# Routing inside the output projection, expert rows scattered per token tile: one change to a Trainium2 hybrid-encoder kernel

## What is computed

```python
def reference(x, meta_tokens, ...):            # x: (1, 1024, 1024) f32, 16 meta tokens in front
    z = rmsnorm(h, attn_norm)
    q, k, v, f_logit, xc, b_gate, c_gate = split(z @ w_in)
    attn = forgetting_attention(q, k, v, f_logit)      # 8 heads of 64
    conv = b_gate * short_conv(c_gate * xc)
    mixed = rmsnorm per group of 64 (concat(attn, conv)) * mix_norm
    h = h + mixed @ w_out
    z = rmsnorm(h, ffn_norm)
    # hierarchical router: top-1 of 4 groups, then top-2 of its 8 experts
    g_prob = softmax(z @ w_rg + b_rg); g_idx = argmax; g_w = max
    top_p, top_i = top_k(softmax((z @ w_re + b_re) of group g_idx), 2); top_p /= sum
    # each expert: (silu(x @ w_gate[e]) * (x @ w_up[e])) @ w_down[e], for the tokens sent to it
    h = h + sum over the two experts of g_w * top_p * expert(z)
    return rmsnorm(h, final_norm)[:, 16:]
```

## Time and profile before

| | |
|---|---|
| median of 3 runs | 1336.21 us (1335.02 to 1337.71) |
| the profiled execution, its own time | 1335.58 us |
| its span, first to last instruction | 1333.8 us |
| PE busy | 1167.0 us, 87% of the span |
| DVE busy | 874.3 us, 66% |
| ACT busy | 737.1 us, 55% |
| POOL busy | 138.8 us, 10% |
| mean granted TensorE clock | 0.95 of full |

### The profile page before, as it was taken

The page is one execution under the profiler, slowest core; times in us unless marked ns, Lnnn a source line. Parts: engine busy times, 40 slices in busy tenths (PEclk is TensorE's granted clock), DMA queues, the critical chain, the costliest instruction groups (busy, mean ns, idle before and its releaser), DMA issues. The chain is left out here.

```text
span 1333.8 us, 17797 instructions
## 1 busy us (share of the span) xinstructions
PE 1167.0 (87%) x6126; PEld 911.4 (68%) x6126; DVE 874.3 (66%) x963; ACT 737.1 (55%) x858; POOL 138.8 (10%) x124
## 2 busy tenths in 40 slices
PE   5999999999999994999519999999999999999940
PEld 4888788778878872788416666666766666676620
DVE  7345535644553554432377888898888889888828
ACT  7343444344444434322116777777777777777713
POOL 0000000000000000101021112222111222221013
PEclk9999999999999997999759999999999999999975
DMA  5201111010111001744349999999999999999728
GB/s 177 63 19 48 48 31 41 22 47 16 48 35 44 17 1 49 248 161 138 131 175 324 375 395 391 398 401 393 397 390 394 395 389 399 400 394 392 312 80 339
DMA packets 78386, 284.08 MB, mean 213 GB/s; under 512 B 12248, under 2 KB 36824, under 8 KB 53776
## 3 DMA queue, kind: packets, MB, share of 16 engines
q1 hardware_dynamic: 66304, 241.04, 47.6%
q0 software_dynamic: 8464, 30.02, 7.1%
q10 hardware_dynamic: 3584, 12.58, 2.4%
HBM read 253.96 MB, written 29.66 MB: 213 GB/s over the span
## 5 line engine op out<-in xcount | busy, mean ns | idle before, releaser
L1436 DVE TENSOR_TENSOR m_wl<-raw,m_wh 128x2048 fp32r<-128x2048 f32 x192 | 437.2, 2289 | 73.9 <-ACT m_wh L1377 71.8
L1377 ACT ACTIVATE m_wh<-raw 128x2048 fp32r<-128x2048 f32 x192 | 367.9, 1918 | 145.3 <-PE m_py L131 50.8
L129 PE MATMUL m_pg<-m_wh,m_xh 128*96 128x512 f32 x256 | 104.5, 408 | 5.7 <-DVE m_xl L1440 4.4
L143 PE MATMUL a_pj<-zh,a_wh 128*128 128x348 f32 (+1 forms) x416 | 107.6, 355 | 0.4 <-DVE a_wl L476 0.4
L143 PE MATMUL a_pj<-zl,a_wh 128*128 128x348 f32 (+1 forms) x416 | 107.6, 355 | 0.0
L143 PE MATMUL a_pj<-zh,a_wl 128*128 128x348 f32 (+1 forms) x416 | 106.4, 352 | 0.0
L129 PE MATMUL m_py<-m_wh,m_hh 128*96 128x512 f32 x256 | 103.1, 403 | 2.3 <-DVE m_hl L1465 2.3
L129 PE MATMUL m_pu<-m_wh,m_xh 128*96 128x512 f32 x256 | 102.6, 401 | 0.0
L131 PE MATMUL m_pg<-m_wh,m_xl 128*96 128x512 f32 x256 | 102.2, 399 | 0.0
L130 PE MATMUL m_pg<-m_wl,m_xh 128*96 128x512 f32 x256 | 101.8, 398 | 0.0
L130 PE MATMUL m_py<-m_wl,m_hh 128*96 128x512 f32 x256 | 101.7, 397 | 0.0
(11 more groups left out here) (271 smaller groups left out, 2132.0 us busy)
## 6 DMA issues: line engine op xcount, KB each, us to landing
raw<-in_w_gate_dram SPq DMA_DIRECT2D x64, 1024.0 KB, 8.2
raw<-in_w_up_dram SPq DMA_DIRECT2D x64, 1024.0 KB, 8.4
raw<-in_w_down_dram SPq DMA_DIRECT2D x64, 1024.0 KB, 7.5
a_raw<-in_w_in_dram SPq DMA_DIRECT2D x24, 512.0 KB, 3.9
yrows<-m_ys ACTq DMA_DIRECT2D x32, 384.0 KB, 7.6
yrows<-o_blank POOLq DMA_DIRECT2D x22, 384.0 KB, 4.5
a_cb<-negcum SPq DMA_DIRECT2D x8, 520.0 KB, 3.8
mx<-in_x_dram SPq DMA_DIRECT2D x8, 512.0 KB, 4.1
```

Source lines behind the costliest of these rows:

```text
L129: nc.tensor.matmul(out, xh, wh, start=first, stop=False)
L143: mm = nc.tensor.matmul(out, w[:, k, 0:m], z[:, k, at:at + n], start=n_pass == 0, stop=n_pass == PASSES - 1)
L1377: nc.scalar.activation(wh[s][:], raw[j][:], ACT.Copy).then_inc(S["w_hi"], 1)
L1436: nc.vector.tensor_tensor(wl[s][:], raw[j][:], wh[s][:].bitcast(F32), ALU.subtract).then_inc(S["w_lo"], 1)
```

## The change

What it does:

- `mixers`: in the last pair the end chain is made in two halves of 512 columns (`sides`). POOL, from the time that the first pair's K is projected, writes zeros to the whole of a new DRAM array `xrows` (expert rows; 50 DMAs of 64 rows) and to the overflow part of `yrows` (33 DMAs of 64 rows), 256 KB each, from a blank piece of `kl`, and waits for them at the block's end.
- `output_projection`: written out for 8 tiles instead of a loop; the table load at its start and the zeroed tile go; the high and low halves of tile 1 move behind four weight pieces. After the logits of a tile DVE makes its routing (`mark`), PE ranks it (`rank`, two small matmuls), DVE makes its slots (`place`) one tile later, and POOL scatters its rows to `xrows` by two indirect DMAs. The first six weight units of the experts are loaded after tile 0.
- `route` goes. The weights, the overflow count and the pairs are made in the first step of `experts` (`settle`); the overflow lists only in the branch for overflow (`lists`, not entered here).
- `experts`: SP waits for all scatters, then loads rows of `xrows` with plain DMAs; the POOL copies and gathers go. The number of overflow pairs is read after the loop.

The diff, cut to its core:

```diff
@@ mixers
+            @block.gpsimd
+            def _(pool):
+                pool.wait_ge(S["blanks_made"], 7)
+                pool.wait_ge(S["projected"], 4)
+                for r in range(0, NE * BLK + P, HD):
+                    pool.dma_start(c.xrows[r:r + HD, :], kl[lower, 1, 0:D].bitcast(F32)).then_inc(c.rows_blanked, 16)
+                for r in range(NE * BLK, NBLK * BLK, HD):
+                    pool.dma_start(c.yrows[r:r + HD, :], kl[lower, 1, 0:D].bitcast(F32)).then_inc(c.rows_blanked, 16)
+                pool.wait_ge(c.rows_blanked, 16 * ((NE * BLK + P + OVB * BLK) // HD))
...
+                    for n, (a, b) in sides(final):
+                        act.wait_ge(S["o_scaled"], i + (n + 1))
+                        nc.scalar.activation(tp[0][:, a:b], o[:, a:b], ACT.Square).then_inc(S["squared"], 1)
+                    for n, (a, b) in sides(final):
+                        act.wait_ge(S["averaged"], i + (n + 1))
+                        nc.scalar.activation(tp[1][:, a:b], s3[:, a:b], ACT.Ln, bias=c.eps[:, 0:1]).then_inc(S["o_ln"], 1)
+                        act.wait_ge(S["o_ln"], i + (n + 1))
+                        nc.scalar.activation(tp[1][:, a:b], tp[1][:, a:b], ACT.Exp, scale=-0.5).then_inc(S["rooted"], 1)
@@ output_projection, DVE
+                def mark(t):
+                    at = slice(t, t + 1)
+                    lg, le = c.logits[:, t, 0:NG], c.logits[:, t, NG:NR]
+                    link(V.tensor_reduce(gmax[:, at], lg, AX.X, ALU.max))
+                    link(V.scalar_tensor_tensor(out=gd[:], in0=lg, scalar=gmax[:, at], in1=down4[:], op0=ALU.is_equal, op1=ALU.mult))
+                    link(V.tensor_reduce(gx[:, at], gd[:], AX.X, ALU.max))
+                    link(V.tensor_scalar(pen[:], down4[:], gx[:, at], NEG, ALU.not_equal, ALU.mult))
+                    link(V.tensor_tensor(masked[0] ..., le ..., pen ..., ALU.add))
+                    for j in range(2):
+                        hot = c.hot[j][:, t, :]
+                        if j == 1:
+                            link(V.scalar_tensor_tensor(out=masked[1][:], in0=c.hot[0][:, t, :], scalar=2 * NEG, in1=masked[0][:],
+                                                        op0=ALU.mult, op1=ALU.add))
+                        link(V.tensor_reduce(emax[j][:, at], masked[j][:], AX.X, ALU.max))
+                        link(V.scalar_tensor_tensor(out=ed[:], in0=masked[j][:], scalar=emax[j][:, at], in1=down32[:],
+                                                    op0=ALU.is_equal, op1=ALU.mult))
+                        link(V.tensor_reduce(at_x[:, t, j:j + 1], ed[:], AX.X, ALU.max))
+                        link(V.tensor_scalar(hot, down32[:], at_x[:, t, j:j + 1], None, ALU.is_equal))
+                    link(V.tensor_tensor(both[:, t, :], c.hot[0][:, t, :], c.hot[1][:, t, :], ALU.add))
+                    link(V.tensor_tensor(c.seen[:, t + 1, :], c.seen[:, t, :], both[:, t, :], ALU.add))
+                    V.tensor_scalar(ngmax[:, at], gmax[:, at], -1.0, None, ALU.mult)
+                    V.tensor_tensor(ediff[:, at], emax[1][:, at], emax[0][:, at], ALU.subtract).then_inc(S["marked"], 1)
+                def place(t):
+                    dve.wait_ge(S["ranked"], t + 1)
+                    rank = pr[:, (t % 2) * NE:(t % 2 + 1) * NE]
+                    for j in range(2):
+                        link(V.tensor_tensor(scratch[:], c.hot[j][:, t, :], rank, ALU.mult))
+                        link(V.tensor_reduce(c.rank[:, j, t:t + 1], scratch[:], AX.X, ALU.add))
+                    r = c.rank[:, :, t]
+                    link(V.scalar_tensor_tensor(out=slot[:], in0=r, scalar=TOP, in1=at_x[:, t, :], op0=ALU.add, op1=ALU.subtract))
+                    link(V.tensor_scalar(late[:], r, BLK - 0.5, 2 * TOP, ALU.is_gt, ALU.mult))
+                    link(V.tensor_tensor(slot[:], slot[:], late[:], ALU.add))
+                    V.tensor_tensor(c.slot_of ..., slot[:], spare[:, t, :], ALU.min).then_inc(S["placed"], 1)
...
+                for t in range(NT):
+                    dve.wait_ge(S["multiplied"], t + 1)
+                    dve.wait_ge(x_in[t % 2], 16 * (t // 2 + 1))
+                    V.tensor_tensor(mix_tile(t), three(xt[t % 2]), three(ph[t % 2]), ALU.add).then_inc(S["h2_done"], 1)
+                    dve.wait_ge(S["rooted"], t + 1)
+                    V.scalar_tensor_tensor(out=by_lane(z2[t % 2]), ...).then_inc(S["z2_done"], 1)
+                    if t + 2 < NT:
+                        mix_low(t + 2)
+                    if t >= 1:
+                        place(t - 1)
+                    dve.wait_ge(S["logits"], t + 1)
+                    link(V.tensor_tensor(c.logits[:, t, :], pl[:, t % 2 * P:t % 2 * P + NR], br[:], ALU.add))
+                    dve.sem_inc(S["logits_out"], 1)
+                    mark(t)
+                place(NT - 1)
@@ output_projection, POOL and ACT
+                for t in range(NT):
+                    pool.wait_ge(S["placed"], t + 1)
+                    for j in range(2):
+                        nc.gpsimd.indirect_dma_start(out=c.xrows[:, :], in_=z2[t % 2][:], in_offset=None, out_offset=...
+                            ).then_inc(c.scattered[t % 2], 16)
...
+                    act.wait_ge(S["h2_done"], t + 1)
+                    if t >= 2:
+                        act.wait_ge(stored[t % 2], 16 * (t // 2))
+                        act.wait_ge(c.scattered[t % 2], 32 * (t // 2))
+                        act.wait_ge(S["turned"], t - 1)
@@ output_projection, PE
+                for t in range(NT):
+                    ahead = t + 1 < NT
+                    if ahead:
...
+                        for k in range(KD):
+                            product(t + 1, k, 0)
+                    if t >= 1:
+                        if t >= 3:
+                            pe.wait_ge(S["placed"], t - 2)
+                        rank(t - 1)
+                    pe.wait_ge(S["z2_done"], t + 1)
...
@@ experts, SP
+                            for s in range(2):
+                                sp.wait_ge(c.scattered[s], 16 * NT)
+                            load_x(0, 0)
+                            load_x(1, 1)
```

More of the change, by code:

```diff
@@ L717, in pair, with average @@
                 def pair(i, final):
[L718 to L722, removed]
+                    def average(sq, done, a=0, b=SEQ):
+                        for at in range(a, b, BANK):
+                            mm = nc.tensor.matmul(s3[:, at:at + BANK], c.blkavg[:], sq[:, at:at + BANK], start=True, stop=True)
                         mm.then_inc(S[done], 1)
@@ L953, in _ @@
+                mix_high(0)
                 for k in range(KD):
                     act.wait_ge(raw_in[k % SLOTS], 16 * (k // SLOTS + 1))
-                    nc.scalar.activation(wh[:, k, :], raw[k % SLOTS][:], ACT.Copy).then_inc(S["w_hi"], 1)
-                with act.Fori(0, ROUNDS - 1) as i:
-                    chain.enter(i, 4)
-                    for n in range(2):
-                        step(i, n, True)
-                chain.leave(ROUNDS - 1)
-                for n in range(2):
-                    step(ROUNDS - 1, n, False)
+                    nc.scalar.activation(wh[:, k, :], raw[k % SLOTS], ACT.Copy).then_inc(S["w_hi"], 1)
+                    if k == 3:
+                        mix_high(1)
@@ L1036, in _, with rank @@
-                pe.sem_inc(S["t_copied"], 1)
-                pe.sem_inc(S["logits_out"], 1)
+                def rank(t):
+                    pe.wait_ge(S["marked"], t + 1)
+                    out = pr[:, (t % 2) * NE:(t % 2 + 1) * NE]
+                    nc.tensor.matmul(out, c.tri[:], both[:, t, :], start=True, stop=False)
+                    nc.tensor.matmul(out, c.ones_bf[:], c.seen[:, t, :], start=False, stop=True).then_inc(S["ranked"], 1)
                 pe.wait_ge(S["m_lo"], 1)
@@ L1347, in step @@
                         sp.dma_start(to, src).then_inc(raw_in[j], 16)
-                rounds(sp, step)
+                rounds(sp, step, lists)
             @block.gpsimd
@@ L1465, in step @@
                         nc.vector.tensor_tensor(hl[:], phid[:, 0:DE // P * BLK], hh[:].bitcast(F32), ALU.subtract).then_inc(S["h_lo"], 1)
-                rounds(dve, step)
+                    if shift == FIRST and not dynamic:
+                        settle()
+                rounds(dve, step, lists)
             @block.tensor
@@ L1493, in into_hidden, with lists @@
                         mm.then_inc(S["unit_used"], 1)
+                def lists(pe):
+                    pe.wait_ge(S["placed"], 1)
+                    for out, values in ((p_lane, token_lane), (p_tile, token_tile)):
+                        for n in range(2 * NT):
+                            mm = nc.tensor.matmul(out[0:BLK, 0:NB], in_row[:, n, :], values[:, n, :], start=n == 0,
+                                                  stop=n == 2 * NT - 1)
+                    mm.then_inc(S["collected"], 1)
+                    pe.wait_ge(S["listed"], 1)
```

(3 more changed lines are left out.)

549 lines of the change are left out of this document (249 added, 300 removed).

## The result

**Slower, by more than the range allowed.** The changed kernel took 1378.55 us (median of 4 executions: 1362.76, 1374.24, 1382.86, 1385.47), the kernel before beside it 1336.06 (1335.02 to 1337.71). The ratio is 1.0283, 95% interval 1.0248 to 1.0318. Ratios here leave out executions that lie more than 1.5% above the fastest of the same kernel (one of these four, one each in experiments 6 and 9, six of twelve in experiment 10), and so, for a kernel whose executions differ as much as this one's, medians are given over all of them. Four further executions gave 1364.34, 1365.79, 1366.99 and 1379.32; the median of all eight is 1370.6.

A forecast was written before the change was run, and what follows sets the result against it. PE was taken to bound the output projection and expert loop, with 40.2 us of routing between them to shorten. Terms -2.7 - 0.5 + 25 + 8 - 20.2 + 1 = +10.6 on 1335.6 gave 1346.2 us; range 1332 to 1357.

The forecast's parts named there:

- Part 1: End of the mixers' last pair: making it in halves shortens the path, -2.7 us (-1.5 to -3.3).
- Part 2: Start of the output projection: table load and second copy leave ACT's front, -0.5 us (0 to -2.3).
- Part 3: Token-tile rounds: `mark` on DVE between logits and next residual stalls PE about 3.5 a round, +25 us (+22 to +28).
- Part 4: Token-tile rounds: PE's clock falls after the gaps, 1.6 us in five of six rounds, +8 (0 to 19).
- Part 5: Last logits to first expert gate matmul: 20.0 us in place of 40.2, -20.2 (-16 to -23).
- Part 6: Mixers: 83 zeroing DMAs, done by 118, meet one nearly late load, +1 us (0 to +3.3).
- Part 7: Expert loop and the rest: plain row loads cost 0; `settle` 0 to 3.4 us, overflow count 0 to +0.9.
- the clock at 2.4 GHz: Rival in the tile rounds: PE's clock stays up despite the gaps, +2.6, 1338.2 us; chance 0.17.
- the short marking: Rival in the tile rounds: `mark` at half price (1.9 us), gaps too short for the clock, 1323.7 us; chance 0.18.
- the scatter: Rival in the tile rounds: ACT's square waits for the scatter of `z2`, +8, 1354 us; chance 0.10.
- "Right" signs: PE idle about 3.5 before transposes, rounds 17.5 to 19, matmuls 0.43 apart, tail about 20, last pair's end 2.7 less.
- "wrong" signs: No gap before transposes, linked instruction at 0.1, ACT released by a DMA, PE waiting for `cb` near 113, tail over 25.

The follow-up runs named there:

- experiment 6: Changed kernel with the marking moved behind the next tile's scaling, slots one tile later still, four `z2` buffers: median 1330.99 us, ratio 0.9990.
- experiment 9: Kernel before with one edit: SP loads the experts' rows among the weights in place of POOL's gather: median 1344.16 us, ratio 1.0045.
- experiment 10: Changed kernel with later marking and paced zeroing, rows loaded by SP before an expert's third weight piece: median 1329.74 us, ratio 0.9891.
- experiment 5: Kernel before with 9 linked, unused vector instructions after the logits of each tile but the last: 1351.17 us, ratio 1.0123.
- experiment 2: Kernel before with only the 83 zeroing DMAs added to the mixers: 1343.19 us, ratio 1.0058.
- experiment 3: Changed kernel with the zeroing paced, one DMA in flight at a time: 1358.43 us, ratio 1.0190.
- experiment 8: Changed kernel with the experts' rows loaded by POOL on its queue instead of by SP among the weights: 1364.38 us, ratio 1.0219.
- experiment 11: Changed kernel with later marking and paced zeroing, experts' rows loaded by POOL on its queue: median 1311.35 us, ratio 0.9820.
- experiment 12: Changed kernel with later marking and paced zeroing, rows loaded by SP before an expert's fifth weight piece: median 1344.82 us, ratio 1.0061.

## Why the prediction was wrong

The sign held, and so did the mechanism of each term that the sum priced; the size did not. 1346.2 was forecast, 1362.76 is the profiled execution, 1378.55 the median. The first 16.6 are sizes of terms. The next 15.8 belong to a term that the sum put at nothing, and how large they come out is a matter of draw: the four further executions have their median 3.6 above 1362.76, all eight 7.9.

- **Part 1**, -2.7: -2.9 in the trace, -2.4 alone. **Part 2**, -0.5: -0.6. Right.
- **Part 3**, marking, +25: 20.6 more of waits in six rounds and 4.1 for tile 7, 24.7. Right, with a small luck in it: the marking is 4.0 rather than 3.75, but the round had not been without a stall before, the six waited 1.8. `place` stayed hidden as argued. Experiment 6 shows that the place made the price.
- **Part 4**, the clock, +8: mis-sized by 9, and the failing step is "five of six rounds with one each, nearest to the row". I took one slow stretch of 1.6 in five of six rounds; it was 2.5 to 2.8 in all six, 16.7 with the little that is not clock. The 1.6 came from a stretch of 3.3 us in the earlier trace rows, behind a gap of 2.53, and was right for gaps of that length: experiment 5 has 1.6 behind 2.1 to 2.7. Behind 3.7 the clock was mostly down before PE began again, so that the transposes paid too: slow from 578.23 to 583.4, a stretch of 5.2. The Trainium skill (TensorE: Matmul & The Clock Gate, "HAM oscillation — how this bites in real kernels") has every burst after a wait throttled again; with gaps of 3.7 the trace agrees, six of six, and with gaps of 2.1 to 2.7 it was four of six.
- **Part 5**, the tail, -20.2: 19.91 in place of 40.15, exact in sum.
- **Part 6**, zeroing, +1: mis-sized by 9, and past its own upper bound of 3.3. The failing step is "at the 395 GB/s of the expert loop": that rate belongs to other transfers, of 1 MB from DRAM into all 128 partitions. The zeroing goes the other way, in pieces of 256 KB, out of 64 partitions; which of these sets its rate no run here separates. These moved at 226 GB/s together with the rest, and kept the DMA engines full through both stretches shown, to 180, not to 118. The second failing step is the upper end, "a doubled landing": 83 DMAs issued in 44 us stood around the bias load, which was 8.3 late instead of 3.3. Experiments 2 and 3 show both the size and that pacing takes nearly all of it away.
- **Part 7**, "the gathers become plain loads of the same bytes ... 0": this is the 15.8. Bytes were the same, the queue was not. The earlier trace rows had the warning: a DMA share of 1.01 through the whole loop. I read from that row that PE sets the time, and did not ask what was left for the DMAs, which is nothing. Experiments 8 and 9 take the edit out and put it in alone; 10 to 12 repeat it. No profile caught a long execution of the changed kernel itself, so that its own long ones lose their time in this loop is inferred from these.

Of the rivals, the clock at 2.4 GHz fell with the 0.83; the short marking with 4.0; the scatter never delayed ACT (it lands in time in every round, and the issue took 0.96, not 2.71). The range was too narrow because every rival moved within the projection, and none in the loop that takes 43% of the time and has its DMAs full. It was also narrower than its own bounds: the upper ones of parts 1 to 6 add up to +32.8, 1368.4, which takes in the profiled execution but not the median. "Right" signs of the last part came as listed, but for rounds of 20.4 instead of up to 19; of the "wrong" signs the one at the bias load came (at 121.92).

**What stays open.** Shown is that the rows' load in the weights' queue makes the loop liable to fall behind, at two places in that queue, in the kernel before as in the changed one, and that POOL's queue does not, in ten executions. Why the DMA engines then move less while they are full, and what decides in one execution and not in the next, isn't settled. Nor is why the same gap of 3.7 costs 1.6 in one round and 2.8 in another.

## What to carry to other kernels

A chain of small linked instructions is priced by what its engine holds up at that place: look for the point where the engine waits for the bound one anyway, and put it there, even at the price of more buffers and a tile's delay. Where an engine that sets the time is full but the DMAs are too, a change of queue is not free; run it several times and look at the slowest executions. Large clears that nobody waits for can go out one at a time: here that took their price from 10.0 to about 0.5.

## What the runs showed of the hardware

- 83 DMAs of 256 KB from SBUF to DRAM, issued back to back, filled the DMA engines (share 0.97) at 226 GB/s and landed after 22.8 and 54.8 us in the median; with one in flight the share was 0.43 to 0.53, and the bias load beside them came 0.9 late instead of 8.3.
- Gaps of 2.1 to 2.2 us before equal work lowered TensorE's clock in two rounds of four; two gaps of 2.6 to 2.7 lowered it both times, and so did every gap of 3.7. The slow stretch cost 1.6 us behind the short gaps and mostly 2.5 to 2.8 behind those of 3.7.
- A full DMA share is not a rate: at a share of 1.02 the same loop moved from 395 down to 355 GB/s, in kernels that differ in the queue and place of a load of 384 KB in about 7 MB an expert.
